# One attention stage rebuilt: which side of a tile's heads is the weight, and who picks the experts

## The reference, cut to what matters

```
s_band = q . k over 128 + 2*128 keys, masked to |k_pos - q_pos| <= 128;  s_ctx = q . kc over 256 keys
p = softmax([sink, s_ctx, s_band]);  o = p_ctx @ vc + p_band @ v          (8 heads, 2 kv heads, head width 64)
mix = concat(rms_norm(att), rms_norm(hy)) @ w_out;   x = x + g1 * mix
h = modulate(rms_norm(x), ...);  group = top-1 of softmax(h @ router_g);  experts = top-2 of 8 inside the group
x = x + g2 * mixture of the two experts' gated products
```

## Time and profile before

| | us |
|---|---|
| median of 3 runs | 2907.66 |
| lowest, highest | 2897.3, 2910.91 |
| the profiled execution: its own time | 2909.62 |
| its span from the first to the last instruction | 2907.9 |
| mean granted clock of TensorE, of 1 | 0.916 |

### The profile page before, as it was taken

One profiled execution on the slowest core, in us unless ns is written; L12 is line 12 of the kernel. 1 busy time (PEld: TensorE's weight loads), 2 busy tenths in 40 slices (PEclk: granted clock), 3 DMA queues, 4 the chain that ended last, 5 costly groups with the idle time before them and its releaser, 6 DMA issues. The chain is left out here.

```text
span 2907.9 us, 45576 instructions
## 1 busy us (share of the span) xinstructions
PE 2491.6 (86%) x15491; PEld 1681.2 (58%) x15492; DVE 1310.2 (45%) x2225; ACT 1101.7 (38%) x2047; POOL 727.6 (25%) x1383
## 2 busy tenths in 40 slices
PE   4887999999959998699999999608888998777997
PEld 1334544444436665589988888505555665544664
DVE  4535473212215554224455444206544665444663
ACT  2542121111124443224454444106444555344562
POOL 1650010000001110512555555531122122221211
PEclk9998999999969998559999999758998999989998
DMA  4983111211173442401111111028876987674893
GB/s 170 314 254 110 31 44 29 73 44 44 29 201 81 118 97 55 120 15 59 59 58 58 58 53 44 30 95 308 283 234 192 348 304 245 225 226 125 297 323 117
DMA packets 238325, 404.73 MB, mean 139 GB/s; under 512 B 24805, under 2 KB 127725, under 8 KB 233413
## 3 DMA queue, kind: packets, MB, share of 16 engines
q1 hardware_dynamic: 160183, 329.28, 33.7%
q0 software_dynamic: 18416, 44.58, 6.6%
q10 hardware_dynamic: 59616, 29.38, 3.7%
HBM read 336.60 MB, written 74.49 MB: 141 GB/s over the span
## 5 line engine op out<-in xcount | busy, mean ns | idle before, releaser
L799 PE MATMUL ps_proj<-sb_hT,sb_win 128*128 128x512 f32 x768 | 336.1, 597 | 7.6 <-DVE sb_rot L904 6.0
L799 PEld LDWEIGHTS ps_proj<-sb_hT,sb_win 128*128 128x128 f32 x768 | 145.7, 192 | 189.9 <-issue 183.0
L2316 PE MATMUL ps_byp<-sb_w,sb_gT 128*128 128x512 f32 x512 | 237.4, 607 | 3.9 <-ACT sb_gT L2131 3.9
L2042 DVE TENSOR_TENSOR sb_w1l<-sb_raw,sb_w1h 128x1024 fp32r<-128x1024 f32 x128 | 148.2, 1220 | 166.3 <-ACT sb_w1h L2103 166.3
L1811 DVE CUSTOM_DVE_ANT_0 sb_pr<-ps_S,sb_mask 128x640 f32<-128x640 f32 x128 | 105.5, 824 | 216.4 <-PE ps_S L1660 216.3
L1346 POOL TENSOR_TENSOR sb_zr<-sb_zr,sb_skip 128x512 f32<-128x512 f32 x32 | 40.0, 1280 | 608.5 <-DMA sb_skip<-in_hy_skip 458.6
L1739 ACT COPY sb_pt<-ps_PT 128x512 f32<-128x512 f32 x128 | 74.7, 584 | 271.4 <-PE ps_PT L1666 271.3
L1680 PE MATMUL ps_O<-sb_v,sb_pt 128*128 128x64 f32 (+1 forms) x1280 | 172.2, 289 | 0.0
L1680 PEld LDWEIGHTS ps_O<-sb_v,sb_pt 128*128 128x128 f32 x1280 | 169.4, 210 | 0.0
L2316 PEld LDWEIGHTS ps_byp<-sb_w,sb_gT 128*128 128x128 f32 x512 | 93.9, 194 | 99.7 <-issue 93.5
L746 PE MATMUL ps_proj<-sb_hT,sb_win 128*128 128x512 f32 x320 | 143.0, 601 | 9.2 <-DMA sb_win<-in_w_in 8.6
(11 more groups left out here) (298 smaller groups left out, 5485.0 us busy)
## 6 DMA issues: line engine op xcount, KB each, us to landing
sb_raw<-in_exp_w SPq DMA_DIRECT2D x64, 2048.0 KB, 15.3
sb_w<-in_exp_w SPq DMA_DIRECT2D x32, 2048.0 KB, 9.9
sb_ada<-in_ada_w SPq DMA_DIRECT2D x16, 1536.0 KB, 8.4
scr_filt<-sb_fout ACTq DMA_DIRECT2D x128, 128.0 KB, 4.4
sb_yh<-scr_filt SPq DMA_DIRECT2D x64, 256.0 KB, 5.0
sb_win<-in_w_in SPq DMA_DIRECT2D x9, 1024.0 KB, 5.6
sb_xr<-in_x SPq DMA_DIRECT2D x16, 512.0 KB, 5.1
sb_gt<-scr_hy_in SPq DMA_DIRECT2D x8, 1024.0 KB, 7.3
```

Of the source, the lines that this page charges most:

```text
L799: ins = pe.matmul(mp[:, (NQ + n) % 4, :], w[:, pc % 3, k, (ct % 2) * P:(ct % 2 + 1) * P], g.hT[:, k, c * 512:(c + 1) * 512], start=(k == 0 ...
L2042: ve.tensor_tensor(piece(low[m], part), piece(raw13[par][:, m], part), piece(high[m], part).bitcast(F32), ALU.subtract).then_inc(lo[m], 1)
L2316: ins = pe.matmul(yp[:, part, :], gT[:, f, :], w2[par][:, f, part * 512:(part + 1) * 512], start=(f == 0), stop=(f == FT - 1), skip_group_ ...
```

## The change

- **Keys.** The key bias is gone; out-of-range keys are masked by three masks (first tile, middle, last). Band keys lie on partitions 0 to 63 of `kT`, context keys on 64 to 127; the query tile is loaded twice, to both halves. Scores are two products of 64 rows, 256 and 384 columns.
- **Values.** `pt` holds all 40 turned blocks of a tile. PE turns them in ten groups of four, one or two groups in a head (`turns`), ACT copies each group in one copy. The products are made in two halves (`tile_values`), after head 3 and after the router: v is the weight (64 columns), the blocks of a kv head's two heads move, the two kv heads go to the two halves of the output partitions. The result is turned back by four transposes (`turn_values`) in the middle of the projection.
- **Picks.** They move from POOL to DVE, one step later, between heads 0 and 3: `pick_group`, `pick_first`, `pick_second`. POOL keeps the products of the picks.
- **Order.** `pr` has one buffer. The heads are taken in the order 0, 4, 1, 5, ... On PE, head 7 stands before the router's product, and the first half of the values is after the transposes of xn. The inverse root of the mixer goes to POOL.
- **w_out** is weighted and split by ACT and DVE between the heads of step 0.
- **Loop.** `pipeline` is written out for all n.

```diff
-    step(Tile(0, -1), True, False, False, False, False)
-    ...
-    with eng.Fori(1, NT // 2 - 1) as j:
-        for off in (1, 2):
-            step(Tile(j, off), True, True, True, True, True)
-    ...
+    for n in range(-1, NT + 3):
+        step(Tile(0, n), n + 1 < NT, 0 <= n < NT, 0 <= n - 1 < NT, 0 <= n - 2 < NT, 0 <= n - 3)
...
-        pr = [e.sb(st, f"pr{b}", [P, NH, KEYS]) for b in range(2)]
+        pr = e.sb(st, "pr", [P, NH, KEYS])
+        pt = e.sb(st, "pt", [P, NH * 5, P])
+        ot = e.sb(st, "ot", [P, NH // 2, P])
...
+        order = [4 * (p % 2) + p // 2 for p in range(NH)]
+        turns = [(0, 1), (2,), (3,), (4,), (5, 6), (7,), (8,), (9,)]
...
 # TensorE
+                def head(p):
+                    if values:
+                        for c in turns[p]:
+                            pe.wait_ge(ex, 8 * t.n + (4 * c + 3) // 5 + 1)
+                            if c == 1:
+                                wait(pe, att, t.n)
+                            else:
+                                wait(pe, tc, 10 * t.n + (c - 1 if c else 0))
+                            for a in range(4):
+                                at = 4 * c + a
+                                ins = pe.transpose(PT[:, (t.par + c) % 2, a * P:(a + 1) * P],
+                                                   pr[:, at // 5, (at % 5) * P:(at % 5 + 1) * P], g.ident[:, :])
+                            ins.then_inc(tp, 1)
                     if scores:
...
+                        wait(pe, sm, 8 * nx.n + p)
...
+                        pe.matmul(S[:, 512 - C:512], qb[nx.par][HD:2 * HD, h, :], g.kT[HD:2 * HD, kv, 0:C],
+                                  start=True, stop=True)
+                        pe.matmul(S[:, 512:512 + 3 * P], qb[nx.par][0:HD, h, :],
+                                  g.kT[0:HD, kv, bass.ds(nx.n * P, 3 * P)], start=True, stop=True).then_inc(qk, 1)
+                def tile_values(half):
+                    pe.wait_ge(tc, 10 * t.n + 5 * half + 5)
+                    ...
                     for a in range(5):
+                        for kv in range(2):
+                            ...
+                            x = pt[:, :, :].rearrange("p (h k a) t -> p k a h t", h=4, k=2)[:, kv, a, 2 * half:2 * half + 2, :]
+                            ins = pe.matmul(OT[kv * HD:(kv + 1) * HD, half, :, :], v, x, start=(a == 0), stop=(a == 4),
+                                            skip_group_check=True)
                     ins.then_inc(pv, 1)
+                def turn_values():
+                    pe.wait_ge(otc, t.n + 1)
+                    pe.wait_ge(tc, 10 * t.n + 9)
+                    for a in range(4):
+                        ins = pe.transpose(PT[:, t.par, a * P:(a + 1) * P], ot[:, a, :], g.ident[:, :])
+                    ins.then_inc(ott, 1)
...
 # VectorE
+                def one_hot(out, x, m, n):
+                    do(ve.scalar_tensor_tensor(out=out, in0=x, scalar=m, in1=rank8[:, 0:n], op0=ALU.is_equal, op1=ALU.mult))
+                    do(ve.tensor_reduce(out=r4[:, pl.par, 9:10], in_=out, axis=AX.X, op=ALU.max))
+                    return ve.tensor_scalar(out, out, r4[:, pl.par, 9:10], None, ALU.is_equal)
...
                 head(0)
                 if route:
                     residual(ro, 1).then_inc(res, 1)
-                for h in range(1, 4):
-                    head(h)
+                if place:
+                    pick_group()
+                head(1)
+                if place:
+                    pick_first()
+                head(2)
+                if place:
+                    pick_second()
+                head(3)
```

More of the change, by code:

```diff
@@ L1535, in _ @@
             pool.memset(powers[:, 1:3], -0.5).then_inc(setup, 1)
-            pool.wait_ge(setup, 8)
+            pool.wait_ge(setup, 6)
             pool.dma_start(g.table.rearrange("(p a) c -> p (a c)", p=P), fill).then_inc(filled, 16)
             pool.wait_ge(filled, 16)
[L1539 to L1548, removed]
             def do(ins):
@@ new lines, in turn_values, with project_half @@
+                def turn_values():
[4 more added lines that the diff above has]
+                    ins.then_inc(ott, 1)
+                def project_half(half):
+                    cs = slice(half * 512, (half + 1) * 512)
+                    for k in range(KT):
+                        pe.matmul(M[:, half, :], mixh[:, k, :], woh[:, k, cs], start=(k == 0), stop=False)
+                        pe.matmul(M[:, half, :], mixh[:, k, :], wol[:, k, cs], start=False, stop=False)
+                        ins = pe.matmul(M[:, half, :], mixl[:, k, :], woh[:, k, cs], start=False, stop=(k == KT - 1))
+                    ins.then_inc(op, 1)
@@ L1686, in step @@
+                for p in range(4):
+                    head(p)
                 if route:
@@ L1706, in step @@
                     ins.then_inc(t1, 1)
+                head(7)
                 if route:
@@ new lines, in head @@
+                        ve.wait_ge(sm, 8 * nx.n + p + 1)
+                        ve.tensor_scalar(nm[:, nx.par, p:p + 1], mx[:, nx.par, p:p + 1], -SCALE,
+                                         nsink[:, order[p]:order[p] + 1], ALU.mult, ALU.min).then_inc(nmx, 1)
+                    if values and isinstance(t.n, int) and t.n == 0:
+                        ve.wait_ge(wo_hi, p + 1)
+                        ve.scalar_tensor_tensor(out=wol[:, p, :], in0=wo[:, p, :], scalar=g.cols[:, C_GN + p:C_GN + p + 1],
+                                                in1=woh[:, p, :].bitcast(F32), op0=ALU.mult, op1=ALU.subtract).then_inc(wo_lo, 1)
@@ L1892, in step @@
                     do(residual(pj, 0))
+                if values:
+                    ve.wait_ge(mxr, t.n + 1)
+                    wait(ve, t1, t.n)
+                    ve.tensor_scalar(mixn[:, 0, :], mix[t.par][:, 0, :], nw[:, 0, 0:1], None, ALU.mult)
+                    ve.tensor_scalar(mixn[:, 1, :], mix[t.par][:, 1, :], nw[:, 0, 1:2], None, ALU.mult).then_inc(mxn, 1)
             pipeline(ve, step)
```

279 lines of the change are left out of this document (126 added, 153 removed).

## The result

The kernel after takes 2919.7 us (median of 7 runs, 2914.2 to 2933.8), the kernel before, run beside it, 2902.5 (7 runs, 2893.0 to 2910.9): a ratio of 1.0069, 95% interval 1.0041 to 1.0097, or some 17 to 20 us more. Forecast were 2944 us and +36 over the runs that were shown then. The direction is right, the size half of what was forecast.

A forecast was written before the change was run, and what follows sets the result against it. TensorE's own work was taken to bound the full steps (37.21 of 37.85 us). Forecast: 2909.6 + 81 (12 steps of +6.7) - 45 (edges) = 2946, less 2.0 for the median: 2944 us, range 2855 to 3020.

The forecast's parts named there:

- The step, +6.7: Each of 12 full attention steps: 41.6 us instead of 37.9 (+3.7), plus 3.0 for the clock, so 44.6.
- The picks: 17 small operations on VectorE between heads 0 to 3, about 0.31 us each: 3.9 us of a full step.
- the clock: Full step: falls to half at about 8 us, returns by the end of the first half of the values: +3.0 us.
- TensorE's own work, 31.8: Full step: TensorE's summed work after the change, 31.8 us from 37.2, through cheaper scores and values.
- rival 3: Full steps: TensorE's sum is the bound, the loop of scores and maximum doesn't bind; -6 a step, 2793 us; chance 0.07.
- rival 2: Full steps: picks hidden, say 0.15 us an operation, clock up; step 37.7, 2863 us; chance 0.20.
- The end, -27: Stage's end: step 15 as now, step 16 -6, the last 55.4 us become 33.5, -21.
- The head, -18: First steps of the attention stage: step -1 -5, step 0 -1, step 1 -12 us.
- the Newton chain: Its replacement by two GpSimd operations was to end well before needed, covered by the projection's 11 us.
- 1: Rival 1, full steps: the clock doesn't fall, no gap reaching 3 us; 2907 us; chance 0.17.
- 4: Rival 4, full steps: the clock falls and returns only in the projection; 3047 us; chance 0.14 together with rival 5.

The follow-up runs named there:

- a1: Kernel after with its 17 pick operations on VectorE moved from between heads 0 to 3 to under the projection of their own step: 2860.7 us, 0.9876 of the kernel before.
- a2: Kernel after with identity transposes into unused PSUM filling TensorE's gaps before heads 2, 3 and the transposes of xn, picks staying: 2890.8 us, 0.9963 of before.
- c2: a1 with the first half of the values ahead of the transposes of xn, and TensorE's left gaps filled by transposes: 2818.6 us, 0.9721 of before.
- b4: Kernel before, steps written out, with only the picks moved to VectorE between heads 0 to 3 and gate exponentials behind head 4: 3090.0 us, ratio 1.0660.
- b3: Kernel before, steps written out, with only the 13 Newton operations on VectorE replaced by two on GpSimd, ahead of the picks: 3032.7 us, ratio 1.0493.
- b2: Kernel before with filler transposes at the start of the attention stage (28) and before each scores of step -1 (8): 2899.1 us, ratio 0.9987.
- d1: Kernel after with value products in the old form (turned exponentials as weights, 64 columns of v moving) at the new place: 3083.2 us, ratio 1.0622.
- d2: Kernel after with both score products of a head on the same 64 rows of the array, one after the other: 3012.6 us, ratio 1.0372.
- a3: Kernel after with TensorE's gaps filled by 10, 7 and 7 real products of the identity with itself: 2889.8 us, 0.9974 of before.

## Why the prediction was half right

- **The step, +6.7.** +6.45 measured (77.4 / 12). The picks 3.8 for 3.9 (a1 against a2), the clock 2.4 for 3.0 (a2), the loops and their order within 0.5 us up to the transposes of xn. Picks and clock are the two terms that make the kernel slower. One row was misread for the clock: the prediction has it come back inside 1815 to 1820, but it was back at 1820.8.
- **TensorE's own work, 31.8.** 33.2 busy in a step at full clock (a1). It isn't the bound, in any run: even c2's step is 36.8, so rival 3 fails. Its 2793 and rival 2's 2863 also lack the 2 us that the forecast takes off for the median.
- **The end, -27.** -26.8: steps 15 and 16 -5.4, the last stretch -21. The reason holds as well: the picks alone gave 24 of it (b4).
- **The head, -18: the step that failed.** It gave -29.4 (steps -1, 0, 1: -7.2, -9.2, -16.3 for -5, -1, -12; step 2 +3.4, for which nothing was forecast). Three terms were wrong. In step 0 the prediction charged all seven loops with the weighting of w_out, 4.3 us each. In the trace the scores of step 0 are 2.5, 4.3, 4.3, then 2.0, 4.3, 4.3 apart, with the first half of the values between: ScalarE and VectorE catch up while TensorE does it. The prediction also put the Newton chain at nothing, as hidden by the projection; step 0 has no projection, and in the kernel before TensorE waited 5.46 us there, of which b3 gave back 2.9. And step 1 was costed at half clock, but the clock was up from about 1239 us; with full clock a loop is 2.0 (1240.65 to 1242.64 in the timeline) for 2.7. The wait before:

```profile
1262.34 1.22 PE L1658 MATMUL ps_S<-sb_kT,sb_qb 65*128 65x256 f32 x2 [5.46 <-DVE sb_mx L1811]
```

Why the old head was slow, b2 and the two d runs show: its mix does not hold the clock there even when it is given (b2), and the old values and the old scores each cost about 14 us. Step -1 came out at -7.2 for another reason than forecast: its loops are 2.73 us as forecast, its first scores 3.1 us later and not 1, and the window of before holds the scores of head 0 of step 0 besides, which the window of after does not.
- **Rivals.** 1: the clock does fall, with gaps of 2.67, 1.92 and 1.99 us. The Trainium skill ("TensorE: Matmul & The Clock Gate", "Why this matters for your kernels") warns there of longer single gaps only; by that rule alone the clock would have stayed up, and the trace does not agree. 2: no pick came under 0.29 us. 4: not in the new mix, but near what the old form of the values does (b4: low for 41 to 44 us a step; d1: mostly 20 to 27). That the change as a whole is nearly neutral rests on that: its picks open gaps that cost the old mix 20 us a step, and its values bring the clock back after 10 us.
- Of the 15 us by which the stage came out below the forecast, 11 are the head's and 4 the steps'. The medians came out another 4 below; that lies outside the stage or in the noise.

What stays open: why the same instructions lose the clock in some steps and keep it in others (a1, 3 of 12 at full clock), why it falls with TensorE fully busy (d1, d2), and how the head's 29 us divide between the shorter work, the cover by the values and the clock.

## What to carry to other kernels

Walk the first, filling steps of a pipeline as carefully as the steady one: work that is hidden by a late part (here the projection) is bare where that part doesn't run yet, and engines that are behind with extra work catch up while another engine has a long block to do. Where small operations move to an engine of a tight loop, look first for a stretch where that engine idles (here 5.8 us under the projection; the move was worth 56 to 59 us by itself). A part of a change tried alone can be far worse than the change: price it with the clock, not only with its length.

## What the hardware showed

- A fully busy TensorE can lose its clock: 1.00 to 0.50 at 2.00 us busy of 2.00, behind the router's products of 36 columns and under values of 64 (d1, 1549 to 1553) or of 256 columns (d2, 1649 to 1651). It can stay low through 36 us at 100% busy (b2, 1206 to 1242). The same mix keeps 1.00 in every full step of the kernel before, where TensorE's only gap is 0.65 us.
- Gaps of 0.56 and 1.24 us went before the fall in b4; the clock was then low for 31 to 44 us.
- Transposes put into the gaps hold the clock (a2) as products do (a3): 1.00 and 41.96 us a step in both.
- Two row-group products start 0.01 us apart and hold TensorE 0.85 us (1534.80 to 1535.65), where one after the other take 1.27 (d2).
